# A bias table in memory with rows of 512 floats for each head, read back as one run of six grid rows

## The reference

```python
dc = col_idx - cols[:, None] + (NA_KC - 1)
rpb_c = rpb.astype(jnp.float32)[:, :, dc]
...
dr = rs + jnp.arange(kr) - r + (NA_KR_MAX - 1)
bias = jnp.transpose(rpb_c[:, dr], (0, 2, 1, 3))
s_loc = jnp.einsum("bwhd,brwkhd->bhwrk", q_r, k_nb).astype(jnp.float32) * scale + bias[None]
```

## Time and profile before

| | us |
|---|---|
| median of 3 runs | 877.16 (876.79 to 877.38) |
| the profiled execution | 883.69 |
| its span | 881.8 |
| TensorE busy in the span | 824.1 |
| VectorE busy | 409.1 |
| ScalarE busy | 240.0 |
| GpSimd busy | 83.1 |

### The profile page before, as it was taken

How to read it: one execution, slowest core, us unless ns; L and a number is a source line. 1 busy time by engine, 2 the same in 40 slices (tenths; PEclk the granted TensorE clock), 3 DMA queues, 4 the chain that set the end, 5 groups by cost and what they waited for, 6 DMA issues and landing times.

```text
span 881.8 us, 17008 instructions
## 1 busy us (share of the span) xinstructions
PE 824.1 (93%) x6978; PEld 524.4 (59%) x6978; DVE 409.1 (46%) x696; ACT 240.0 (27%) x449; POOL 83.1 (9%) x155
## 2 busy tenths in 40 slices
PE   5897999999899999999996899979899999999993
PEld 2587996569655455554542888559555455554541
DVE  0476798656822323223336643457822323223334
ACT  3752443543211111111113532442211111111102
POOL 4171000021000000000000344200000000000000
PEclk9999998699899999999998999989999999999996
DMA  9999795688999999999996986599999999999981
GB/s 357 367 270 321 257 381 168 211 247 306 408 409 408 409 408 408 409 400 410 409 409 242 315 216 200 149 372 335 373 395 409 409 409 408 409 409 408 409 349 50
DMA packets 109393, 300.60 MB, mean 341 GB/s; under 512 B 12577, under 2 KB 43585, under 8 KB 109305
## 3 DMA queue, kind: packets, MB, share of 16 engines
q1 hardware_dynamic: 102592, 286.53, 86.3%
q0 software_dynamic: 6384, 12.76, 5.2%
q10 hardware_dynamic: 328, 0.11, 0.0%
HBM read 291.77 MB, written 2.92 MB: 334 GB/s over the span
## 4 chain that ended last, share of the span: by engine, by line
PE 77%; DMA 12%; DVE 6%; ACT 3%; issue 2%; SPq 0%; DVEq 0%; ACTq 0%
PE ps L2147 25%; PE ps L2172 12%; PE ps L2098 5%; DMA slots<-in_w_mod 4%; DMA slots<-in_moe_w 3%; PE ps L2234 3%; PE ps L2068 3%; PE ps L1702 3%; DMA slots<-in_na_w_in 2%; PE ps L2069 2%; PE ps L2260 2%; PE ps L2261 2%; PE ps L2262 2%; PE ps L1915 1%; PE ps L1828 1%
## 5 line engine op out<-in xcount | busy, mean ns | idle before, releaser
L2147 PE MATMUL ps<-slots,xg 128*64 128x256 f32 (+1 forms) x2432 | 248.7, 384 | 1.7 <-DMA slots<-in_moe_w 1.7
L2147 PEld LDWEIGHTS ps<-slots,xg 128*64 128x64 f32 (+1 forms) x2432 | 133.1, 128 | 88.5 <-issue 28.8
L1551 DVE SCALAR_TENSOR_TENSOR xres<-ps,gs,xres 128x512 f32<-128x512 f32 x128 | 90.0, 747 | 171.6 <-PE ps L2098 171.6
L2172 PE MATMUL ps<-slots,hidT 128*64 128x512 f32 (+1 forms) x608 | 117.1, 596 | 0.9 <-ACT hidT L1028 0.5
L1139 DVE TENSOR_TENSOR wlo<-slots,whi 128x1024 fp32r<-128x1024 f32 x56 | 66.7, 1220 | 14.5 <-ACT whi L828 14.1
L2172 PEld LDWEIGHTS ps<-slots,hidT 128*64 128x64 f32 (+1 forms) x608 | 34.1, 128 | 64.5 <-issue 61.8
L828 ACT CAST whi<-slots 128x1024 fp32r<-128x1024 f32 x56 | 56.8, 1046 | 55.4 <-DMA slots<-in_na_w_in 38.4
L1702 PE MATMUL ps<-slots,pair 128*32 128x256 f32 x576 | 48.0, 450 | 10.5 <-DMA slots<-in_w_mod 7.1
L1535 DVE TENSOR_TENSOR yg<-ps,g2keep 128x512 f32<-128x512 f32 x32 | 21.5, 689 | 71.4 <-PE ps L2172 71.4
L1009 ACT COPY xg<-ps 128x384 f32<-128x384 f32 (+2 forms) x44 | 20.6, 469 | 123.8 <-PE ps L2069 114.7
L1022 ACT ACTIVATE silu<-ps 128x256 f32<-128x256 f32 x32 | 11.6, 382 | 116.0 <-PE ps L2147 116.0
(11 more groups left out here) (285 smaller groups left out, 1331.3 us busy)
## 6 DMA issues: line engine op xcount, KB each, us to landing
slots<-in_moe_w SPq DMA_DIRECT2D x384, 512.0 KB, 15.1
slots<-in_w_mod SPq DMA_DIRECT2D x96, 512.0 KB, 8.2
slots<-in_na_w_in SPq DMA_DIRECT2D x24, 512.0 KB, 9.6
slots<-in_cf_pw_w SPq DMA_DIRECT2D x24, 512.0 KB, 8.8
slots<-in_ab_w_out SPq DMA_DIRECT2D x8, 512.0 KB, 4.6
mods<-mod_scratch POOLq DMA_DIRECT2D x8, 512.0 KB, 8.6
urep<-uT SPq DMA_DIRECT2D x64, 35.5 KB, 3.7
urep<-uT POOLq DMA_DIRECT2D x64, 35.5 KB, 3.6
```

The costliest lines, as they stand in the source:

```text
L1551: V.scalar_tensor_tensor(out=dst, in0=ps[:, plan.spread_banks(m, i)[half], :], scalar=gs[:, t, place:place + 1], in1=dst, op0=ALU.mult, op ...
L2147: ins = T.matmul(ps[lo:lo + width, BW[a], c0:c0 + 2 * P], tile[:, k, o:o + width], raw[:, p.slot(u), w0:w0 + 2 * P], start=(q == 0 and kk ...
L2172: ins = T.matmul(ps[lo:lo + width, BY[a], :], hidT[:, a, o:o + width], raw[:, p.slot(u), half * HALF:(half + 1) * HALF], start=(q == 0), s ...
```

## The change

`rpbt` becomes 8 partitions, one for each head, with a row of 512 floats in which the seven row offsets stand at a pitch of 64. One transfer loads it. The table in memory becomes 8 x 64 rows of 512 floats (2 KB), 1.05 MB for 1.84 MB. Each head is read back by 2 transfers of 64 partitions with one run of 384 floats (1536 bytes) for each, six row offsets. The tile `bias` has 384 floats for a head and partition, 12 KB in all, over slots 2 to 4 of `mods`; each half of the tokens takes its 256 columns at its own start, so they overlap. The mask is added to 384 columns. As heads 6 and 7 now lie in slot 4, GpSimd waits for the last maximum before it fills that slot. `stage`, the neighbour of `rpbt`, moves by 1.5 KB.

```diff
-        rpbt = at("rpbt", [HEADS * 7, P], 48)
+        rpbt = at("rpbt", [HEADS, BAND], 48)
...
-        bias = at("bias", [P, HEADS, NT, SEQ], 2 * D * 4 / 1024, base=mods_at)
+        bias = at("bias", [P, HEADS, NEAR * GRID_W], 2 * D * 4 / 1024, base=mods_at)
...
-            for h in range(HEADS):
-                eng.dma_start(rpbt[h * 7:(h + 1) * 7, 48:48 + 2 * KCOL - 1], na_rpb[0, h, 4:11, :]).then_inc(rpb_in, 16)
-            eng.wait_ge(rpb_in, 16 * HEADS)
+            bands = rpbt[:, GRID_W - KCOL:GRID_W - KCOL + OFFS * GRID_W].rearrange("h (r c) -> h r c", r=OFFS)[:, :, 0:2 * KCOL - 1]
+            eng.dma_start(bands, na_rpb[0, :, 4:4 + OFFS, :]).then_inc(rpb_in, 16)
+            eng.wait_ge(rpb_in, 16)
             eng.wait_ge(tensor_unit, 2 * KC)
-            eng.dma_start(bias_scratch, rpbt[:].unsqueeze(1).broadcast_to([HEADS * 7, GRID_W, P])).then_inc(rpb_out, 16)
+            eng.dma_start(bias_scratch, rpbt[:].unsqueeze(1).broadcast_to([HEADS, GRID_W, BAND])).then_inc(rpb_out, 16)
             def load_bias(h):
-                for t in range(NT):
-                    for half in range(2):
-                        src = bass.AP(tensor=bias_scratch.tensor, offset=(h * 7 + 3 - 2 * t - half) * GRID_W * P + GRID_W - 1,
-                                      ap=[[P - 1, GRID_W], [GRID_W * P, ROWS], [1, GRID_W]])
-                        dst = bias[half * GRID_W:(half + 1) * GRID_W, h, t, :].rearrange("p (r c) -> p r c", r=ROWS)
-                        eng.dma_start(dst, src).then_inc(bias_in[h // 2], 16)
+                for half in range(2):
+                    src = bass.AP(tensor=bias_scratch.tensor, offset=h * GRID_W * BAND + (1 - half) * GRID_W + GRID_W - 1,
+                                  ap=[[BAND - 1, GRID_W], [1, NEAR * GRID_W]])
+                    eng.dma_start(bias[half * GRID_W:(half + 1) * GRID_W, h, :], src).then_inc(bias_in[h // 2], 16)
...
             for v in range(2, 5):
+                if v == 4:
+                    eng.wait_ge(biased, 2 * HEADS)
                 mod_fill(v, mods[:, v * D:(v + 1) * D])
...
-                eng.wait_ge(bias_in[h // 2], 128)
-                full = bias[:, h].rearrange("p t (r c) -> p (t r) c", r=ROWS)
-                mask = cst[:, C_MASK:C_MASK + GRID_W].unsqueeze(1).broadcast_to([P, NT * ROWS, GRID_W])
+                eng.wait_ge(bias_in[h // 2], 64)
+                full = bias[:, h].rearrange("p (r c) -> p r c", r=NEAR)
+                mask = cst[:, C_MASK:C_MASK + GRID_W].unsqueeze(1).broadcast_to([P, NEAR, GRID_W])
...
-                link(V.tensor_tensor(local, local, bias[:, h, t, :], ALU.add))
+                link(V.tensor_tensor(local, local, bias[:, h, 2 * (1 - t) * GRID_W:2 * (1 - t) * GRID_W + SEQ], ALU.add))
```

More of the change, by code:

```diff
@@ L22 @@
 ROWS = SEQ // GRID_W
+OFFS = 2 * ROWS - 1
+NEAR = OFFS - 1
+BAND = 8 * GRID_W
 HEADS = 8
@@ L389, in program @@
         early = at("early", [R_EARLY, P], 0)
-        stage = at("stage", [R_N - R_EARLY, P], 48.5)
+        stage = at("stage", [R_N - R_EARLY, P], 50)
         early_rows = at("early_rows", [P, 2, QW], 20)
@@ L2390 @@
     args.append(nc.dram_tensor("in_consts", [P, C_N], F32, kind="ExternalInput").ap())
-    args.append(nc.dram_tensor("bias_scratch", [HEADS * 7, GRID_W, P], F32, kind="Internal").ap())
+    args.append(nc.dram_tensor("bias_scratch", [HEADS, GRID_W, BAND], F32, kind="Internal").ap())
     args.append(nc.dram_tensor("mod_scratch", [MODS, D], F32, kind="Internal").ap())
```

## The result

The changed kernel took **882.42 us** (median of 4 runs, 881.02 to 885.13), the kernel before 876.97 beside it: a ratio of 1.0065 (95% interval 1.0039 to 1.0091). A later repeat gave 1.0046 (1.0031 to 1.0062). The prediction said 872.0, with a range up to 877.5: wrong, in sign too.

The account below looks back on a forecast made before the run. TensorE's work, with a 6.2 us gap waiting on unit 9, was the bound; -8.8 (read) and +4.2 (write) closed it, less 1.1 for margin: -5.1, masks -0.1, total -5.2, median 872.0 us, range 870.3 to 877.5.

Parts of the forecast that it names:

- The bound of before: TensorE's work bounds 62 to 140 us; its gap at the value tiles is the only loss, 6.2 us at most.
- Rival (d): Weights come too late for the earlier TensorE behind 91.4, half the gain arrives: 874.5 us; 0.11, shared with smaller gains.
- Part 2, the write: Writing the table from 8 partitions: lands at 56.1, 5.9 us later, by a geometric middle; puts off 4.2 us of weights.
- Each us puts off 0.71 us: Each us that the table's write lasts longer delays 0.71 us of SyncE's weight traffic, from 109 against 382 GB/s.
- (b): Rival: the write takes 24 us, lands near 62.5 and eats the gain: 877 us, no change; chance 0.14.
- (c): Rival: the 8-partition write becomes the bound; landing at 70 gives 882.4 us, far end 893 or more; chance 0.13.
- SyncE's queue is not starved of anything that TensorE needs by 62: Weights ahead of the value tiles: no loss below the write's delay, as units 2 to 5 are rounded from 47.2 on.
- a new wait for `kT` near 68: Sign of being wrong: TensorE waits in the key tiles because ScalarE rounds units 6 and 7 late; no size given.
- Part 1, the read back: Reading the table back in 16 transfers of 1536 byte pieces: unit 9 lands 8.8 us sooner, at least 2.1.
- As cheap as weight pieces: Read-back pieces would cost what weight pieces do: 382 GB/s instead of 252, so 13.1 us instead of 21.9.
- Part 3 and 4: VectorE's masks on 384 columns, about 0.56 us each: -0.1 us; small edits such as the wait on `biased`: nothing.
- (a): Rival: the write is not slowed, or SyncE's traffic passes it, and the gap vanishes: 870.9 us; chance 0.22.

Follow-up runs that it names:

- slow_write_256: Changed kernel's write from partitions 0 to 7, with 256 byte reads back and the larger tile and masks of the kernel before: 887.18 us, 1.0132.
- stride4: Changed kernel with its eight source rows spread over partitions 0, 4, ... 28 instead of 0 to 7: 870.18 us, 0.9919; repeated, 869.34 us, 0.9902.
- before_112: Kernel before, with its rows held twice, on 112 partitions, each read 32 times; old layout, reads and tile: 872.2 us, 0.9961.
- copies2: Changed kernel with each row held twice, on 16 neighbouring partitions, each read 32 times: 869.29 us, 0.9919.

## Why the prediction was wrong

**The bound of before, right.** The most that TensorE can get back was put at 6.2 us. Spread rows give 91.23 - 85.16 = 6.1 at the first query matmul, and 6.3 and 7.2 us in the two medians, so it passes to the end whole. Rival (d) falls.

**Part 2, the write, is the step that failed.** Its landing was nearly right: 56.1 forecast, 58.0 measured. Its price was not: 4.2 us of lateness for unit 9, where slow_write_256 shows 11.3.
- The landing was near by luck. The geometric middle of 6.6 and 46 us stands for no mechanism; it was taken because neither end had a nearer row. The Trainium skill, "SBUF — State Buffer", section on the DMA port swizzle, did give a nearer figure: an estimate from its 27.6 GB/s for a port has 19 us by two ports and a landing at 57.7 (32.3 + 6.4 + 19). The trace agrees in kind, with 24 GB/s for four neighbouring partitions in two kernels; that the landing itself agrees to 0.3 us is partly chance, since 1.05 MB at twice 24 GB/s would be some 22 us, which leaves 4 of the 25.7 and not 6.4 for start and receipt.
- "Each us puts off 0.71 us" is the term that was mis-sized. It counts the bytes that SyncE's queue loses, and lets them be caught up at 382 GB/s, as if the queue then had the engines alone. The bytes were right: from 34 to 58 us the queue moved 4.85 MB before, 2.72 in the change and 2.80 in slow_write_256, some 2.1 MB less, and a landing 7.8 us later in the change, 8.6 in slow_write_256 (58.8), gives 2.1 to 2.3 MB at the forecast's 273 GB/s. But behind a late write come the reads of the table, and they run while the queue catches up: from 58 to 88 us it moved 5.56 MB in slow_write_256, 185 GB/s. At that rate 2.05 MB are 11.1 us, an estimate, against the 11.3 measured: 1.3 us for each us of lateness, not 0.71. Rows of `q1` (before, change, slow_write_256 for 34 to 58 us, then slow_write_256 for 58 to 88):

```profile
q1 hardware_dynamic: 3309, 4.85, 65.3%
...
q1 hardware_dynamic: 2017, 2.72, 34.7%
...
q1 hardware_dynamic: 2074, 2.80, 35.8%
...
q1 hardware_dynamic: 3248, 5.56, 69.7%
```

- The prediction did not see SyncE's issue stand still for 19.32 us either. The Trainium skill, "DMA: Bandwidth & Descriptors", section on why a DMA increments its semaphore by 16, expects 8 engines for this transfer; 44.5% of 16 agrees with that, though no row names engines. I had set that rule beside rivals (b) and (c), and not asked what the other eight would be able to finish.
- "SyncE's queue is not starved of anything that TensorE needs by 62" looked at units 2 to 5 only. In truth unit 5 slipped as well, from inside the row of four roundings at 47.2 to 59.95, and unit 7 became the gate. The prediction names that place among the signs of being wrong (a new wait for `kT` near 68, ScalarE's rounding of units 6 and 7 late), and gives it no price. It is where TensorE's wait of 6.83 us stands.

**Part 1, the read back, was right in direction.** 8.8 us forecast for unit 9, 6.2 measured with the slow write. "As cheap as weight pieces" fails: 252 GB/s were expected to become 382, and 58 to 75 us show 276. The destination of 64 partitions keeps them at 68 ns for each KB (44 at 128 partitions); what was gained are a quarter of the bytes and a seventh of the price.

**Sum.** -8.8 + 4.2 was forecast for unit 9, and it came out at -6.5 + 11.3 = +4.9 (76.69 to 81.56; here the read term is the difference of the two profiles, 88.03 - 81.56). Through the earlier gate, TensorE lost 3.1 us more in the gap than before.

**Part 3 and 4, right.** The masks take 0.55 us for the 0.56 forecast. The new wait on `biased` shows, and is hidden behind the wait for `mrow` as said. Timeline of POOL after (as the earlier trace rows):

```profile
186.27 0.53 POOL L740 DMA_DIRECT2D mods<-mod_scratch  x1 [2.29 <-DVE smx L1316]
...
196.44 0.61 POOL L734 DMA_DIRECT2D mod_scratch<-mrow  x1 [4.58 <-DVE mrow L1196]
```

**The rivals.** (c) gave 882.4, the number measured, but for a landing at 70 and through unit 9; the write landed at 58, below (c)'s threshold of 62.6, and still cost this much. That its number came true is luck. (a) is what stride4 is: the write not slowed, 870.9 forecast, 870.18 measured. The 0.13 for slower was too little: the slope that set its threshold was the weakest number in the text.

## What to carry to other kernels

Count the groups of four neighbouring partitions that a transfer's SBUF side touches before merging rows: eight source rows at a step of 4 cost 152 ns a packet, side by side 608. The count is not the whole rule: 2 groups moved 49 GB/s, 4 moved 97, 8 moved 178 (stride4) and 28 moved 310 (before_112), but the 14 groups of the kernel before only 177 (0.53 MB in 43 to 46 us), no more than 8. A slow transfer's price is what it does to the other queues on the engines that it holds, and that can begin with their issue; read it from who was issued or landed late, and ask what else will run while they catch up. In an engine that works in order, look which copy stands behind each load that may be late: every such pair is a gate of its own, and pricing only the one that binds today misses the next.

## What the runs showed of the hardware

- Two issues on SyncE stood for 16.7 to 19.3 us in all five profiles with the slow write (6.18 with spread rows) while GpSimd's transfer ran: traffic of one queue can hold the issue of another.
- With 86.2% of 16 engines busy on four groups of four partitions (copies2) a packet took 552 ns, with 44.5% on two groups 608.
- Reading from memory to 64 partitions with every engine busy moved 256 GB/s in all; the same pieces to 128 partitions, beside more of SyncE's traffic, 367 in all.
- The granted clock fell for some 3 us near 44 in TensorE's key tiles, in all five profiles with the slow write, and in before_112; not in that of the kernel before, nor in the seven others. The work of TensorE up to there is the same in before and after: idle for 1.9 us until 42.1, then busy. Window 44 to 48 us, before, after and then before_112:

```profile
44.00:48.00 4.00, 4.00 (x18) 3.20 (x17) 2.93 (x9) 3.97 (x8) 0.00 (x0) 1.00 0.96 220
44.00:48.00 4.00, 4.00 (x13) 3.11 (x12) 2.95 (x9) 3.97 (x8) 0.00 (x0) 0.63 0.50 67
44.00:48.00 4.00, 4.00 (x13) 3.18 (x12) 3.08 (x9) 3.97 (x8) 1.15 (x2) 0.63 1.05 353
```

18 matmuls were done there before, 13 after: the 1.4 us that TensorE is late at 63.41. As before_112 has the fall at 353 GB/s and without the slow write, that write isn't needed for it. Five of five profiles with the slow write against one of nine without it make a link likely, but none is shown, so whether it belongs to the change stays open, and so does how often the unprofiled runs of the kernel before have it; the other 3.1 us of the 4.46 don't hang on it.

Open too: why the attention of before's profiled execution ran at clock 0.76; and how the 19 us of blocked issue divide between the engines held and the order in the queues, as no row tells single engines apart.
